# Softmax normalisation of the attention blocks moved from ScalarE to VectorE, in a fused two-block transformer kernel on one core

## The reference, cut to what matters

```
def block(args):
    qn, qr = args                      # 128 query tokens of every head
    sc = (jnp.einsum("bqhd,bkhd->bhqk", qn, k_nope)
          + jnp.einsum("bqhr,bkr->bhqk", qr, k_rope))
    p = jax.nn.softmax(sc.astype(jnp.float32) * scale, axis=-1).astype(v.dtype)
    return jnp.einsum("bhqk,bkhd->bqhd", p, v)
```

```
y = jnp.concatenate([y_attn, u], axis=-1) @ w_o[l]
```

## Time and profile before

| | before |
|---|---|
| median of 3 runs | 2155.96 us (2154.66 to 2157.46) |
| the profiled execution | 2155.96 us, span 2154.2 us |
| PE busy | 1953.8 us, 91% |
| DVE busy | 1210.7 us, 56% |
| ACT busy | 1048.6 us, 49% |
| POOL busy | 289.6 us, 13% |
| granted clock of PE, mean | 0.959 |

### The profile page before, as it was taken

One profiled execution on the slowest core, in us unless ns is written; L12 is line 12 of the kernel. 1 busy time (PEld: TensorE's weight loads), 2 busy tenths in 40 slices (PEclk: granted clock), 3 DMA queues, 4 the chain that ended last, 5 costly groups with the idle time before them and its releaser, 6 DMA issues. The chain is left out here.

```text
span 2154.2 us, 26197 instructions
## 1 busy us (share of the span) xinstructions
PE 1953.8 (91%) x8323; PEld 1552.4 (72%) x8323; DVE 1210.7 (56%) x1894; ACT 1048.6 (49%) x1871; POOL 289.6 (13%) x216
## 2 busy tenths in 40 slices
PE   7999989889999988767799999999968799999997
PEld 6777768668878867645487888787745477888786
DVE  4443356453333346898466666536697566575634
ACT  4554464334343333579654344434469754343432
POOL 0001000010000001267310000001257501000000
PEclk8999989999999999979999999999979999999999
DMA  3122112223323222211023333223210023333222
GB/s 126 48 68 63 58 39 84 78 69 97 98 88 98 97 74 67 56 25 35 23 90 89 98 97 98 93 97 83 67 32 30 15 79 89 102 91 104 94 95 81
DMA packets 148116, 162.29 MB, mean 75 GB/s; under 512 B 34104, under 2 KB 102670, under 8 KB 148044
## 3 DMA queue, kind: packets, MB, share of 16 engines
q1 hardware_dynamic: 148044, 161.38, 24.9%
HBM read 159.24 MB, written 2.10 MB: 75 GB/s over the span
## 5 line engine op out<-in xcount | busy, mean ns | idle before, releaser
L1210 DVE TENSOR_TENSOR w_lo<-w_raw,w_hi 128x512 fp32r<-128x512 f32 (+3 forms) x617 | 442.2, 726 | 738.1 <-ACT w_hi L931 413.5
L931 ACT ACTIVATE w_hi<-w_raw 128x512 fp32r<-128x512 f32 (+3 forms) x392 | 232.3, 603 | 446.5 <-PE bank_b L1845 227.4
L1843 PE MATMUL bank_b<-h_hi,w_hi 128*128 128x512 f32 x816 | 321.9, 394 | 4.4 <-DVE var L1228 3.9
L1843 PE MATMUL bank_a<-h_hi,w_hi 128*128 128x512 f32 x720 | 285.1, 396 | 40.4 <-DVE h_lo L1213 20.4
L1845 PE MATMUL bank_b<-h_hi,w_lo 128*128 128x512 f32 x816 | 318.8, 391 | 0.0
L1844 PE MATMUL bank_b<-h_lo,w_hi 128*128 128x512 f32 x816 | 318.7, 391 | 0.0
L709 ACT ACTIVATE w_hi<-w_raw 128x512 fp32r<-128x512 f32 x225 | 140.5, 631 | 327.1 <-PE bank_a L1845 180.6
L1844 PE MATMUL bank_a<-h_lo,w_hi 128*128 128x512 f32 x720 | 283.8, 394 | 0.0
L1845 PE MATMUL bank_a<-h_hi,w_lo 128*128 128x512 f32 x720 | 283.6, 394 | 0.0
L1213 DVE SCALAR_TENSOR_TENSOR arena<-arena,cols_all 128x512 f32<-128x512 f32 x272 | 221.8, 865 | 0.0
L1843 PE MATMUL bank_a<-split,w_hi 128*128 128x512 f32 x420 | 169.3, 403 | 33.8 <-DVE split L1210 25.6
(11 more groups left out here) (234 smaller groups left out, 2709.2 us busy)
## 6 DMA issues: line engine op xcount, KB each, us to landing
w_raw<-in_w_up_dram SPq DMA_DIRECT2D x240, 256.0 KB, 3.1
w_raw<-in_w_down_dram SPq DMA_DIRECT2D x152, 256.0 KB, 2.8
w_raw<-in_w_in_dram SPq DMA_DIRECT2D x64, 256.0 KB, 2.9
w_raw<-in_w_gate_dram SPq DMA_DIRECT2D x32, 256.0 KB, 2.6
w_raw<-in_w_o_dram SPq DMA_DIRECT2D x32, 256.0 KB, 2.8
w_raw<-in_w_out_dram SPq DMA_DIRECT2D x16, 256.0 KB, 2.9
w_raw<-in_w_in_dram SPq DMA_DIRECT2D x16, 192.0 KB, 2.4
w_raw<-in_w_in_dram SPq DMA_DIRECT2D x16, 144.0 KB, 2.1
```

What stands on the lines that cost most here:

```text
L931: nc.scalar.activation(w_hi[:, s, 0:c], w_raw[:, s, 0:c], ACT.Copy).then_inc(w_round, 1)
L1210: return nc.vector.tensor_tensor(out_, a, b, op)
L1843: nc.tensor.matmul(out_, a_hi, b_hi, start=start, stop=False, skip_group_check=loose)
```

## The change

The multiplication by the reciprocal is taken out of ACT's turn and put into DVE's turn, right behind the reciprocal. It becomes a tensor_scalar of the same 128x512 block, in place, with a wait for the reciprocal (p_step) on DVE itself. It signals the same semaphore, p_ready, for which PE waits before its transposes. Nothing else is changed; semaphore counts, buffers and the order of everything else stay.

```
--- before.py
+++ after.py
@@ -1059,12 +1059,6 @@
                         act.wait_ge(mx_step, was[mx_step.name] + g + 1)
                         nc.scalar.activation(prob[:, b, :], s_banks[g % 2], ACT.Exp,
                                              bias=soft[:, 1, b:b + 1], accum_out=soft[:, 2, b:b + 1]).then_inc(p_exp, 1)
-                    if 1 <= g <= BLOCKS:
-
-                        b = (g - 1) % TT
-                        act.wait_ge(p_step, was[p_step.name] + g)
-                        nc.scalar.activation(prob[:, b, :], prob[:, b, :], ACT.Copy,
-                                             scale=soft[:, 3, b:b + 1]).then_inc(p_ready, 1)
                     if g >= 2:
 
                         b = (g - 2) % TT
@@ -1701,6 +1695,9 @@
                         b = (g - 1) % TT
                         dve.wait_ge(p_exp, was[p_exp.name] + g)
                         nc.vector.reciprocal(soft[:, 3, b:b + 1], soft[:, 2, b:b + 1]).then_inc(p_step, 1)
+                        dve.wait_ge(p_step, was[p_step.name] + g)
+                        nc.vector.tensor_scalar(prob[:, b, :], prob[:, b, :], soft[:, 3, b:b + 1], None,
+                                                ALU.mult).then_inc(p_ready, 1)
                     taps(taps_by(g) - tap)
                     if i + 1 < PAIRS:
                         if m == 4:
```

More of the change, by code:

```diff
@@ L1061, in _ @@
                                              bias=soft[:, 1, b:b + 1], accum_out=soft[:, 2, b:b + 1]).then_inc(p_exp, 1)
[L1062 to L1067, removed]
                     if g >= 2:
```

## The result

The changed kernel takes 2168.81 us (median of four runs, 2167.78 to 2169.55) against 2156.06 us before (the three runs above and a fourth): 12.7 us slower, a ratio of 1.0058 with a 95% interval of 1.0041 to 1.0077. Forecast were 2148 us and a gain. The time is outside the stated range, 2138 to 2164, and nearest to rival (b), 2164.

What follows compares the result with a forecast made beforehand. ACT was taken to bound most of the two attention stages, DVE their first pair. The terms gave -5.1 us a layer, +1.2 for old holds, net -3.9, -7.8 in both: 2156 - 8 = 2148 us, range 2138 to 2164.

Steps and rivals of the forecast that it cites:

- rival (b): Attention stages: new holds by POOL additions raise the price to 1.0 us a normalisation; 8 us slower, 2164 us; chance 0.24.
- What bounds the kernel: Two attention stages: ACT sets the pace except in the first pair, where DVE does; the rest only shifts.
- What ACT loses: Attention stages: each normalisation frees 0.61 us of ACT, 19.5 us in each layer.
- The bare price: DVE in the attention stages: 0.40 us for an unheld normalisation, nothing for waiting on its own reciprocal.
- The port price: DVE beside POOL additions: 0.25 us of hold in all, making 0.65 us for one normalisation.
- the cheap place: DVE right behind maximum and reciprocal, about 0.7 us without shared operands, where a running POOL addition comes nearer its end.
- The nine taps of the prediction: Taps behind the reciprocal from 939.26 to 1021.88: mean 0.87 us, so 0.15 us of hold.
- The rule of the Trainium skill: DVE and GpSimd share a port: the second waits until the first is done; by this alone, 2164 us.
- The sum: Attention stage: pairs +2.8, -2.6, -0.8, then -2.4 and -2.1, old holds +1.2; net -3.9 us a layer.
- The 1.2 us a layer for the old holds: Attention stages: existing holds come 5% more often, as POOL does the same work in a shorter time: +1.2 us.
- (a): Attention stages: DVE takes over the bound at a price of about 0.83 us; no gain, 2156 us; chance 0.21.
- The signs: Changed profile: wrong in size above 0.83 us growth; in kind if DVE under 90% busy or PE still waits 24.7 us.

Runs made afterwards that it cites:

- the 32-column pair: GpSimd's product additions cut from 512 to 32 columns, in the kernel before and in the changed kernel: 2131.07 us without the change, 2109.14 us with it.
- the 256-column pair: GpSimd's product additions cut from 512 to 256 columns, in the kernel before and in the changed kernel: 2135.55 us without the change, 2121.09 us with it.
- the reduce: Changed kernel with the new tensor_scalar replaced by a tensor_reduce over 310 columns of the same block, normalisation left out: 2151.89 us, ratio 0.9982 to before.

## Why the prediction was wrong, point by point

- *What bounds the kernel.* Right: ACT in three quarters of the stage, DVE in the first pair; only the attention stages moved. Without most of the holds, but with the same work on ACT (109.44 us), the stage fell only to 115.12 us.
- *What ACT loses.* Right: 0.61 us each was said; 109.62 to 92.02 us in the stage, 0.59 each.
- *The bare price.* Too low. I took 0.40 us and nothing for DVE's wait on its own reciprocal, since every tap waits for the one before it and still overlaps. That reading of the kernel was wrong, here and in its description: two sums alternate, and a tap waits by tap_done for the tap before last, never for the one in front of it. With additions of 32 columns the price is 0.55 us. The lost overlap explains 0.08 of the 0.15; another 0.05 is the mean of 0.532 us there against the 0.48 that I took. The gap of 0.03 us is idle time and comes on top.
- *The port price.* This is the step that failed: "so most holds change owner and few are new", 0.25 us. Measured in the first layer were 0.43 us for each, 13.1 us a stage, of which only some 5 us lie on the new instruction itself (27 x (0.717 - 0.53), with 0.53 us its mean beside 32-column additions). The rest is on taps and remainders that had been there before, and I had counted 1.2 us for these. The new instruction did get the cheap place, as I said; but the tap that it pushed back went from 0.96 to 1.26 us, 22 times in a stage. The nine taps of the prediction, with a mean of 0.87, were those that stand alone in their turn; all 22 right behind a reciprocal have 0.96, and the taps behind them 1.47, which I hadn't read. The premise, one hold at most for each addition, was not refuted. That many additions had run while DVE was idle or at work on PSUM, and now meet a shared instruction, fits all this and is not shown by itself.
- *The rule of the Trainium skill* (SBUF — State Buffer, "Who interferes with whom"), that the second one "fully blocks": the trace agrees, with four held rows in sequence. As a rule that speaks against the change it had its price in rival (b), 1.0 us for each normalisation. Measured were 0.98 and 1.16.
- *The sum.* Its form holds, with one term too small. DVE's growth in the three full pairs, over the normalisations in them:

| layer, pair | stage, before and after, us | DVE busy, before and after, us | for each normalisation, us |
|---|---|---|---|
| 1, first | 31.63, 35.18 | 29.06, 34.10 | 0.72 |
| 1, second | 32.14, 34.43 | 23.58, 33.28 | 1.21 |
| 1, third | 33.64, 36.67 | 26.86, 36.09 | 1.15 |
| 2, first | 30.27, 35.17 | 25.82, 34.09 | 1.18 |
| 2, second | 32.13, 34.28 | 23.92, 33.17 | 1.16 |
| 2, third | 33.66, 38.69 | 26.87, 37.36 | 1.31 |

That is 1.04 us each over the pairs of the first layer and 1.22 of the second, where I had 0.65. Put into my sum, which gave -0.6 us for the three pairs, they give 8.4 and 12.5 us; measured were 8.9 and 12.1. The 1.2 us a layer for the old holds must then go, since these prices contain them. The last eight blocks, up to PE's products of L2228, were forecast at -4.5 us and gave -3.8 and -3.9. In all that makes 11.9 us instead of -8, and 12.7 were measured. The price is no constant of the instruction: the two first pairs end at the same load, 34.1 us, and came from 29.06 and 25.82. Why these two differed before the change I didn't test.
- *The rivals.* (b) had the price, but put the decision into the first pair, at 36.9 us; that pair came to 35.2 us in both layers, and the second and third pair got longer too, where a gain was forecast. (a) had the mean hold of all taps, 0.44, as its condition, which is almost what the first layer shows; with the bare price of 0.40 it came out at no change.
- *The signs.* By the prediction's own words it is wrong in the size, since new and old shared instructions grew by more than 0.83 us for each normalisation, and not in its kind: DVE is busy for over 96% of the first three pairs, and PE waited 12.9 us for the block and not 24.7.

Shown by runs: that GpSimd's additions turn the sign (the 32-column pair), that it is not their number but their length, or the time it fills (the 256-column pair), and that the loss needs an instruction that they hold (the reduce). Only argued: how the 0.15 us of the bare price divide, and why the price differs from pair to pair.

## What to carry to other kernels

Where one engine is held by another through a shared resource, price a moved instruction at the mean hold that its neighbours show now, or above it, and add the holds that its neighbours get when it pushes them back; the place right behind unshared work spares only the first of them (0.96 us for that tap here, 1.47 for the one behind it). Then compare the whole load of the receiving engine with the length of the stage that the relieved one sets. And when a normalisation meets a transpose by a matrix product, fold it into the matrix: a 128x128 diagonal instead of a 128x512 block was a gain of 0.4% here, on the engine whose rows show no hold (0.387 to 0.413 us for all 32).

## What the runs showed of the hardware that was not expected

- The time that DVE loses to GpSimd depends strongly on the length of the additions, at the same count: with 32, 256 and 512 columns DVE's same 137 instructions of the stage took 71.63, 74.91 and 91.55 us before the change. From 256 to 512 columns POOL's busy time in the stage grew by 60%, from 53.91 to 86.37 us, and DVE's excess over the 32-column kernel from 3.3 to 19.9 us, six times.
- Making the held instruction four times smaller saved 0.11 of 0.72 us; without holds it would have saved 0.20 (0.286 against 0.485 us).
- A tensor_reduce with one input in SBUF was not held once in 30 times beside full additions (0.475 to 0.478 us).
- A DVE instruction that waits for the DVE instruction in front of it (the normalisation for the reciprocal, all 64 times) started 0.03 to 0.04 us after its end; in the attention stages the taps, which wait for the tap before last, start 0.07 to 0.09 us before the end of the row in front of them.
